# Two transformer blocks on one core: in seven FFNs, gate and up blocks as seven block products in place of eight, with weight sums made by adding transfers

## What is computed

```python
def swiglu(x, w_gate, w_up, w_down):
    return (jax.nn.silu(x @ w_gate) * (x @ w_up)) @ w_down

for l in range(DEPTH):
    x = x + 0.5 * swiglu(rmsnorm(x, ffn1_norm[l]), ffn1_w_gate[l], ffn1_w_up[l], ffn1_w_down[l])
    x = x + hybrid_mixer(rmsnorm(x, mix_norm[l]), ...)
    x = x + 0.5 * swiglu(rmsnorm(x, ffn2_norm[l]), ffn2_w_gate[l], ffn2_w_up[l], ffn2_w_down[l])
```

## Time and profile before

| | us |
|---|---|
| median of 3 runs | 2456.77 (2456.68 to 2456.95) |
| profiled execution, span | 2455.0 |
| PE busy | 2426.3 (99%) |
| DVE busy | 1559.7 (64%) |
| ACT busy | 1183.0 (48%) |
| POOL busy | 205.5 (8%) |
| SP's queue, 433.23 MB | 49.2% of 16 DMA engines |
| POOL's queue, 67.65 MB | 8.6% of 16 DMA engines |

### The profile page before, as it was taken

One profiled execution on the slowest core, in us unless ns is written; L12 is line 12 of the kernel. 1 busy time (PEld: TensorE's weight loads), 2 busy tenths in 40 slices (PEclk: granted clock), 3 DMA queues, 4 the chain that ended last, 5 costly groups with the idle time before them and its releaser, 6 DMA issues.

```text
span 2455.0 us, 30703 instructions
## 1 busy us (share of the span) xinstructions
PE 2426.3 (99%) x12690; PEld 2069.7 (84%) x12690; DVE 1559.7 (64%) x1629; ACT 1183.0 (48%) x1276; POOL 205.5 (8%) x358
## 2 busy tenths in 40 slices
PE   8999999999999999999999999999999999999998
PEld 6889998888889988888889878888888898788887
DVE  6555876655656776565558657656665677577664
ACT  5435544434437544444435664544344356644442
POOL 0100200100100101101100010011011000100010
PEclk9999999999999999999999999999999999999999
DMA  8755447657654447657664445476576454454762
GB/s 334 238 209 189 156 165 246 227 209 237 236 204 181 164 148 272 227 205 259 227 214 174 161 154 206 180 262 231 202 256 231 172 184 152 150 208 159 256 232 101
DMA packets 82547, 504.42 MB, mean 205 GB/s; under 512 B 11608, under 2 KB 12760, under 8 KB 30184
## 3 DMA queue, kind: packets, MB, share of 16 engines
q1 hardware_dynamic: 61488, 433.23, 49.2%
q0 software_dynamic: 19744, 67.65, 8.6%
q10 hardware_dynamic: 1176, 1.58, 0.4%
HBM read 476.72 MB, written 25.69 MB: 205 GB/s over the span
## 4 chain that ended last, share of the span: by engine, by line
PE 91%; DVE 5%; ACT 3%; issue 1%; DMA 1%; SPq 0%; POOL 0%; DVEq 0%; POOLq 0%; ACTq 0%
PE acc L615 24%; PE acc L616 24%; PE acc L617 24%; PE acc L583 4%; PE acc L584 4%; PE acc L585 4%; DVE w_lo L516 2%; PE aux L799 1%; ACT w_hi L508 1%; DMA raw<-in_w 1%; ACT tmp L1484 1%; PE stat L633 1%; PE bc L633 0%; PE aux L1170 0%; PE aux L981 0%
## 5 line engine op out<-in xcount | busy, mean ns | idle before, releaser
L516 DVE TENSOR_TENSOR w_lo<-raw,w_hi 128x2048 fp32r<-128x2048 f32 (+1 forms) x417 | 934.3, 2244 | 672.3 <-ACT w_hi L508 671.5
L508 ACT ACTIVATE w_hi<-raw 128x2048 fp32r<-128x2048 f32 (+1 forms) x417 | 782.8, 1880 | 624.2 <-PE acc L617 594.0
L615 PE MATMUL acc<-w_hi,x_hi 128*128 128x512 f32 (+1 forms) x1848 | 720.4, 390 | 3.1 <-DVE x_lo L1736 2.1
L617 PE MATMUL acc<-w_lo,x_hi 128*128 128x512 f32 (+1 forms) x1848 | 715.6, 387 | 0.0
L616 PE MATMUL acc<-w_hi,x_lo 128*128 128x512 f32 (+1 forms) x1848 | 715.5, 387 | 0.0
L615 PEld LDWEIGHTS acc<-w_hi,x_hi 128*128 128x128 f32 x1848 | 347.1, 188 | 77.8 <-issue 6.1
L617 PEld LDWEIGHTS acc<-w_lo,x_hi 128*128 128x128 f32 x1848 | 347.0, 188 | 71.3
L616 PEld LDWEIGHTS acc<-w_hi,x_lo 128*128 128x128 f32 x1848 | 347.2, 188 | 70.4 <-issue 1.0
L615 PE MATMUL acc<-w_hi,h_parts 128*128 128x512 f32 x704 | 274.5, 390 | 0.0
L617 PE MATMUL acc<-w_lo,h_parts 128*128 128x512 f32 x704 | 273.9, 389 | 0.0
L616 PE MATMUL acc<-w_hi,h_parts 128*128 128x512 f32 x704 | 273.9, 389 | 0.0
(11 more groups left out here) (396 smaller groups left out, 2229.3 us busy)
## 6 DMA issues: line engine op xcount, KB each, us to landing
raw<-in_w SPq DMA_DIRECT2D x399, 1024.0 KB, 4.8
squares<-tmp POOLq DMA_DIRECT2D x40, 512.0 KB, 2.9
tmp<-squares POOLq DMA_DIRECT2D x160, 128.0 KB, 4.5
raw<-in_w SPq DMA_DIRECT2D x18, 512.0 KB, 3.6
tmp<-in_norm_gb POOLq DMA_DIRECT2D x8, 1024.0 KB, 5.4
tmp<-in_norm_gb POOLq DMA_DIRECT2D x6, 512.0 KB, 3.7
tmp<-in_gate_rows POOLq DMA_DIRECT2D x12, 256.0 KB, 3.1
squares<-tmp POOLq DMA_DIRECT2D x8, 256.0 KB, 2.3
```

The source lines that it names most:

```text
L508: nc.scalar.activation(w_hi[:, slot, 0:kind], raw[:, slot, 0:kind], ACT.Copy).then_inc(hi_done, 1)
L516: nc.vector.tensor_tensor(w_lo[:, slot, 0:kind], raw[:, slot, 0:kind], w_hi[:, slot, 0:kind].bitcast(F32), ALU.subtract).then_inc(lo_done, 1)
L615: nc.tensor.matmul(out, vh, wh, start=first and k == 0, stop=False)
L617: last = nc.tensor.matmul(out, vh, wl, start=False, stop=last_k and k == nk - 1)
```

## The change

In every FFN but the first, blocks 1 and 2 form a group, and blocks 3 and 4 another. Write X as four blocks, X11 and X12 (tokens 0 to 127, rows 0 to 511 and 512 to 1023 of the weights) and X21 and X22 (the other tokens), and the weights of the first block of the group as B11, B21 (gate) and B12, B22 (up). The 2 x 2 product takes eight block products; the group takes seven, each 12 matmuls of 512 columns (`product`): X11 B11, X12 B21, X22 T4, and products of the weight sums T1 = B12 + B11, T2 = T1 + B22, T3 = B22 + B12 and of B22 with four sums of x, where T4 = T2 + B21. The group's second block is done as before, its four chunks laid between the products. A group has eleven chunks (T1, B11, B22, gate 0, T2, B21, T3, gate 1, T4, up 0, up 1) in place of eight; PE works 180 matmuls for it in place of 192.

The four sums of x are X21 - X22 (for T1), X21 - X22 - X11 (T2), X11 - X21 (T3) and X12 + X21 - X22 - X11 (B22).

The weight sums are made by transfers: POOL issues a DMA that adds a weight chunk to what lies in the `raw` buffer. T2 is added onto T1 and T4 onto T2, T3 onto B22, each once the old content has been split; SP skips those chunks. T1 is a load and then an add.

The sums of x: POOL adds `x_hi` and `x_lo` and forms the four sums (`x_sums`, eight operations of 128x512), ACT rounds each (`sum_high`), DVE writes the remainder (`sum_low`). PE accumulates the products in the banks of `aux` and `bc`, where ACT and DVE copy and subtract in between (`kept`). Some semaphores are merged to make room.

```diff
-FFN = [WIDE] * (UP_CHUNKS + 5) + [HALF] * 2 + [WIDE] * 5
-SUBS = ["ffn", "mix1", "ffn"] * 2 + ["ffn", "mix2", "cross", "ffn"] * 2
-KINDS = {"ffn": FFN, "mix1": MIX1, "mix2": MIX2, "cross": CROSS}
-TILES = {"ffn": 26, "mix1": 30, "mix2": 46, "cross": 10}
+FFN0 = [WIDE] * (UP_CHUNKS + 5) + [HALF] * 2 + [WIDE] * 5
+FFN = [WIDE] * (UP_CHUNKS + 6 + 5) + [HALF] * 2 + [WIDE] * 5
+SUBS = ["ffn0", "mix1", "ffn"] + ["ffn", "mix1", "ffn"] + ["ffn", "mix2", "cross", "ffn"] * 2
...
+B11, B21, B12, B22 = range(4)
+GROUP = (((LOAD, B12), (ADD, B11)), ((LOAD, B11),), ((LOAD, B22),), ((LOAD, 4 + B11),),
+         ((ADD, B22),), ((LOAD, B21),), ((ADD, B12),), ((LOAD, 4 + B21),),
+         ((ADD, B21),), ((LOAD, 4 + B12),), ((LOAD, 4 + B22),))
+G_T1, G_B11, G_B22, G_GATE0, G_T2, G_B21, G_T3, G_GATE1, G_T4, G_UP0, G_UP1 = range(11)
+GROUPS = ((1, 4), (3, 15))
...
+            if moves[c][-1][0] == ADD:
+                act.wait_ge(added[sums.index(c) % 2], 16 * (sums.index(c) // 2 + 1))
+            else:
+                act.wait_ge(loaded[slot], 16 * landings[c])
...
+                how, place = moves[c][0]
+                if how == ADD:
+                    continue
...
+                def product(c, bank, v_hi, v_lo, first):
+                    chunk_ready(c)
+                    for k in range(4):
+                        wh, wl = wblock(c % RING, k, 512)
+                        nc.tensor.matmul(bank, v_hi[:, k], wh, start=first and k == 0, stop=False, skip_group_check=True)
+                        nc.tensor.matmul(bank, v_lo[:, k], wh, start=False, stop=False, skip_group_check=True)
+                        last = nc.tensor.matmul(bank, v_hi[:, k], wl, start=False, stop=k == 3, skip_group_check=True)
+                    last.then_inc(chunk_done, 1)
+                def group(g, b, tile):
+                    a_, b_, e_ = aux[:, 0, :], aux[:, 1, :], bc[:, :]
+                    x11, x12, _, x22 = ((x_hi[:, k, at], x_lo[:, k, at]) for k, at in X_AT)
+                    s1, s3, s2, s4 = zip(SUM_HI, SUM_LO)
+                    pe.wait_ge(sum_parts, 4 * (f - 1) + 1)
+                    if b:
+                        pe.wait_ge(outs_ready, 3 * b - 2)
+                    product(g + G_T1, e_, *s1, True)
+                    if b:
+                        pe.wait_ge(kept_silu, 2 * b)
+                    product(g + G_B11, b_, *x11, True)
+                    pe.wait_ge(sum_parts, 4 * f)
+                    pe.wait_ge(kept_copied, 3 * b + 1)
+                    product(g + G_B22, e_, *s4, False)
+                    both(g + G_GATE0, tile, 0)
+                    pe.wait_ge(kept_copied, 3 * b + 2)
+                    product(g + G_T2, b_, *s2, False)
+                    if b:
+                        pe.wait_ge(outs_ready, 3 * b - 1)
+                    product(g + G_B21, a_, *x12, True)
+                    pe.wait_ge(kept_copied, 3 * b + 3)
+                    product(g + G_T3, b_, *s3, False)
+                    both(g + G_GATE1, tile, 1)
+                    pe.wait_ge(outs_ready, 3 * b + 3)
+                    product(g + G_T4, b_, *x22, False)
+                    both(g + G_UP0, tile + 2, 0)
+                    both(g + G_UP1, tile + 2, 1)
                 if s:
                     skewed_in(s, c0, t0)
-                for j in range(4 if s else 0, UP_CHUNKS):
-                    both(c0 + j, t0 + 2 * (j // 2), j % 2)
-                    if s == 6 and j == 8:
-                        bias_rows()
+                    for n, (i, g) in enumerate(GROUPS):
+                        group(c0 + g, 2 * (f - 1) + n, t0 + 4 + 4 * n)
+                        if s == 6 and n == 0:
+                            bias_rows()
+                    for j in range(2):
...
+                def sum_high(q):
+                    act.wait_ge(sum_ready, 4 * (f - 1) + q + 1)
+                    nc.scalar.activation(SUM_HI[q], XQ4[SUM_AT[q]], ACT.Copy).then_inc(sum_hi, 1)
+                def kept(g, b, i):
+                    ended_chunk(act, g + G_T1)
+                    act.wait_ge(sum_parts, 4 * f)
+                    if i > 1:
+                        act.wait_ge(hid_ready, 12 * f + 2 * (i - 2) + 2)
+                    nc.scalar.activation(Q5B, bc[:, :], ACT.Copy).then_inc(kept_copied, 1)
+                    ahead.to(g + 4)
+                    ended_chunk(act, g + G_B11)
+                    nc.scalar.activation(P1B, aux[:, 1, :], ACT.Copy).then_inc(kept_copied, 1)
+                    ahead.to(g + 5)
                     if i > 1:
                         hid_high(i - 2)
-                    silu(i, 0)
-                    silu(i, 1)
-                    for j in range(1, 4 if i < 5 else 2):
-                        if s == 6 and i == 2 and j == 1:
-                            bias_copy()
-                        ahead.to(c0 + 4 * i + j + 4)
+                    ahead.to(g + 7)
+                    ended_chunk(act, g + G_T2)
+                    nc.scalar.activation(UB, aux[:, 1, :], ACT.Copy).then_inc(kept_copied, 1)
+                    ahead.to(g + 9)
+                    act.wait_ge(outs_ready, 3 * b + 2)
+                    nc.scalar.activation(P1B, P1B, ACT.Silu).then_inc(kept_silu, 1)
+                    ahead.to(g + 10)
+                    hid_high(i - 1)
+                    silu(i + 1, 0)
+                    silu(i + 1, 1)
+                    ahead.to(g + 11)
+                    ended_chunk(act, g + G_T4)
+                    nc.scalar.activation(G1B, aux[:, 1, :], ACT.Silu).then_inc(kept_silu, 1)
+                    ahead.to(g + 14)
+                def ups():
+                    if s == 0:
+                        ahead.to(c0 + 4)
+                    silu(0, 0)
+                    if s:
+                        sum_high(0)
+                    ahead.to(c0 + 4)
+                    if s:
+                        for q in range(1, 4):
+                            sum_high(q)
+                    silu(0, 1)
+                    ahead.to(c0 + 7)
+                    if s:
+                        for n, (i, g) in enumerate(GROUPS):
+                            kept(c0 + g, 2 * (f - 1) + n, i)
+                            if s == 6 and n == 0:
+                                bias_copy()
+                        return
...
+                def sum_low(q):
+                    dve.wait_ge(sum_hi, 4 * (f - 1) + q + 1)
+                    V_.tensor_tensor(SUM_LO[q], XQ4[SUM_AT[q]], SUM_HI[q].bitcast(F32), ALU.subtract).then_inc(sum_parts, 1)
+                def kept_times(i, tt, gates_, ups_, ready):
+                    n = 12 * f + 2 * i + tt
+                    dve.wait_ge(squares_ready, n - 1)
+                    dve.wait_ge(*ready)
+                    V_.tensor_tensor(HID[:, tt], gates_, ups_, ALU.mult).then_inc(hid_ready, 1)
+                    dve.wait_ge(hid_ready, n + 1)
+                def kept(g, b, i):
+                    ahead.to(g + 4)
                     if i > 1:
                         hid_low(i - 2)
-                    if i < 5:
+                    ahead.to(g + 7)
+                    dve.wait_ge(kept_copied, 3 * b + 3)
+                    V_.tensor_tensor(UB, bc[:, :], UB, ALU.subtract).then_inc(outs_ready, 1)
+                    ahead.to(g + 8)
+                    ended_chunk(dve, g + G_B21)
+                    dve.wait_ge(kept_copied, 3 * b + 2)
+                    V_.tensor_tensor(P1B, P1B, aux[:, 0, :], ALU.add).then_inc(outs_ready, 1)
+                    ahead.to(g + 9)
+                    ended_chunk(dve, g + G_T3)
+                    dve.wait_ge(kept_copied, 3 * b + 1)
+                    V_.tensor_tensor(Q5B, Q5B, aux[:, 1, :], ALU.subtract).then_inc(outs_ready, 1)
+                    dve.wait_ge(outs_ready, 3 * b + 1)
+                    kept_times(i, 0, P1B, UB, (kept_silu, 2 * b + 1))
+                    ahead.to(g + 10)
+                    hid_low(i - 1)
+                    ahead.to(g + 11)
+                    dve.wait_ge(outs_ready, 3 * b + 3)
+                    kept_times(i, 1, G1B, Q5B, (kept_silu, 2 * b + 2))
+                    turn_squares(i)
+                    ahead.to(g + 13)
+                    times(i + 1, 0)
+                    times(i + 1, 1)
+                    turn_squares(i + 1)
+                    ahead.to(g + 14)
+                def ups():
+                    if s == 0:
+                        ahead.to(c0 + 6)
+                    times(0, 0)
+                    if s:
+                        sum_low(0)
+                        ahead.to(c0 + 4)
+                        for q in range(1, 4):
+                            sum_low(q)
+                    ahead.to(c0 + 6)
+                    times(0, 1)
+                    turn_squares(0)
+                    ahead.to(c0 + 7)
+                    if s:
+                        for n, (i, g) in enumerate(GROUPS):
+                            kept(c0 + g, 2 * (f - 1) + n, i)
...
+            def add(c):
+                how, place = moves[c][-1]
+                if len(moves[c]) > 1:
```

(47 more changed lines are left out.)

209 lines of the change are left out of this document (135 added, 74 removed).

## The result

The changed kernel takes **2715.84 us** (median of 4 runs, 2711.21 to 2723.45) against 2456.72: a ratio of 1.1058, 95% interval 1.1044 to 1.1071. I had forecast 2474 with a range up to 2511. Slower was right, the size was not: 259 us are lost, not 17.

The account below looks back on a forecast made before the run. TensorE was taken as the bound (busy 2426.3 of 2455.0 us). -38.1 + 7 x (5.4 + 1.2 + 1.1) + 1.6 = +17.4 gave a span of 2472.4, plus 1.8 for the runs' median: 2474 us, range 2438 to 2511.

Parts of the forecast that it names:

- The matmuls: TensorE over seven FFNs: 168 fewer matmuls at 0.2267 us each save 38.1 us, a span of 2416.9 with nothing else.
- The start of the first group: Each FFN: POOL's sums of x delay chunk 5's split, so PE waits 5.4 us after T1.
- The 1.2 us in front of chunk 7: First ordinary chunk of each FFN's first group: DVE has 6.6 us of work against PE's 5.44, costing 1.2 us.
- 1.6 once: FFN of sublayer 6: three more transfers issued ahead of its sums of x cost 1.6 us once.
- The adding transfers: An add lands after 7.7 us; T4's costs 1.1 us per FFN in the first group, nothing in the second.
- T1 and T3 of the second group: No cost: T2 and T3 have 9 us and more, T1's add comes some 10 us before ACT wants it.
- Rival A: Adds move bytes twice and land after 9.6 us, delaying T4: 2497 us, 2511 at 10.6; chance with beyond 0.20.
- The sign that I gave for being wrong: Wrong on the adds if ACT never waits for DMA at T2 or T4, or several microseconds in every group.
- B: Start of the first group: the sums of x hide, both waits go, the whole 38.1 is won: 2419 us; chance 0.10.
- C: POOL is not held by DVE and adds are as cheap as loads: 2447 us; chance 0.14.
- D: Gain and waits cancel within 5 us, with T4 in time: 2457 us; chance 0.14.

Follow-up runs that it names:

- run 6: The changed kernel with its 56 adding transfers left out (weight sums missing), sums of x still on POOL: 2468.28 us.
- run 7: run 6 with the sums of x on VectorE and the splits of chunks 5 and 6 moved ahead: 2417.71 us.
- run 2: The changed kernel with its adding transfers overwriting instead of adding, in the same places (weight sums missing): 2597.55 us.
- Run 4: The changed kernel with the squares' store on SP's queue, ahead of the load of a later chunk: 2637.49 us.
- run 5: The changed kernel with T4's add ahead of the permutation, sums of x on VectorE and the squares' store on SP's queue: 2589.52 us.
- run 8: run 5 with the 56 transfers overwriting instead of adding (weight sums missing): 2494.35 us.
- 10: The changed kernel with T1 by load and adding transfer (14 adds), the other weight sums and the sums of x on VectorE: 2510.9 us.
- 12: 10 with T1 by adding transfer in the first group only (7 adds), by VectorE in the second: 2466.45 us.
- run 1: The changed kernel with T4's add issued ahead of the permutation in both groups: 2629.71 us.
- 13: 12 with VectorE splitting the second group's B11 earlier: 2472.41 us.
- 14: 12 with the transposes of the squares behind the next ordinary chunk's split, at the start of both groups: 2466.84 us.
- 15: 14 with POOL forming the low halves of three blocks' hidden values: 2471.45 us.
- run 11: 10 with two of the eight operations of the sums of x on POOL: 2518.07 us.

## Why the prediction was wrong, step by step

- **The matmuls: right.** -38.1 forecast; without adds and with VectorE's sums the span is 2416.0, forecast 2416.9 for "nothing else". (The pages count 12690 and 12522 matmuls, 168 fewer, as the listing does.)
- **The start of the first group: the wait right, the total partly by luck.** POOL's operations take 1.29 us alone and up to 3.33 beside a low split, as worked out from the earlier trace rows, and PE waits for chunk 5's low split: 5.4 us forecast, 4.8 measured. The 1.2 us in front of chunk 7 never show. Behind the wait PE ran at the low clock, so B11's matmuls took from 394.97 to 399.21, 4.2 us in place of 2.72, and chunk 7's low split (the first of two in 4.45 us from 399.10) was in time. Forecast 47.8 us (7 x 6.6 and 1.6 once), measured 50.6 by runs 6 and 7: 18.0 us of it are longer busy time, which I had priced at nothing, and it fills the place of what the waits lack.
- **The adding transfers: the failed step.** 7 x 1.1 = 7.7 us forecast, 247.5 measured. PE's wait in front of T4 was to be 1.1 us in the first group and nothing in the second; it is 11.4 to 16.1 us in both. Four things in it were wrong. *(a) Its landing:* 7.7 us taken, at most 10.6. T4's adds take 13.2 to 15.5. The price of adding doesn't explain that: plain, in the same place, they take 13.8 (run 2), while the other plain ones mostly land after 5 to 6. I priced a transfer by itself and not among the four loads ahead of it on its queue and SP's loads beside it. *(b) What stands ahead of it:* I gave the squares' store 2.9 to 4.9 us. It lands after 9.7 to 14.7, since T3's add lies in front of it on its queue and in the DMA engines, and T4's add is issued only then. Run 4 alone gives 78 us back. I counted that add's cost to ACT and not to what stands behind it. *(c) The bytes:* I compared 360 GB/s (463 with adds counted twice) with 420 and let the run-ahead of eight chunks carry the rest. Runs 5, 8 and 7 show 95 us for adding and 77 us for the bytes, with the order of run 5. *(d) The clock:* I counted a wait at its length. Behind the waits TensorE's clock was down: its busy time is 61.5 us longer than its matmuls need, 43.6 of it with the adds (2449.7 against 2406.1 in run 6).
- **T1 and T3 of the second group: not priced.** I gave T2 and T3 "9 us and more"; the add of the second group's T3 lands after 11.2 to 11.5 us, and PE waits 14.7 us for it over seven FFNs. I wrote that T1's add comes "some 10 us before ACT wants it", which holds for the first group alone; runs 10 and 12 put 44 us on the second's.
- **Rival A** had the direction and half of the mechanism (an add takes the engines nearly twice as long), but the wrong size (2497 to 2511): it kept the issue times of a queue in which nothing is late. The sign that I gave for being wrong, ACT waiting for DMA several microseconds in every group, is what the waits show (328.6 us, 53 times).
- **B, C and D** are out. B wanted POOL's sums to hide; run 6 has them without adds and loses 50.6 us. B's bound of 2419, no wait at all, is reached with VectorE's sums (run 7, 2417.7). C wanted POOL unheld and adds as quick as loads, and neither is so. D wanted gain and waits to cancel within 5 us: even without adds run 6 is 11.4 us above the kernel before.

What stays open: which of its neighbours make T4's transfer so late. Ahead of the squares' loads a plain one takes 8.1 to 10.9 us (run 8, where the store is on SP's queue as well), an adding one still 12.1 to 16.0 (run 1). How the 77 us of plain transfers divide between bandwidth and the order in which they go out was not taken apart. That VectorE's amount of work bounds 12 is argued from its busy time and from 13 to 15; no run had less of it without using POOL.

## What to carry to other kernels

A transfer inside a chain (a store that its reader waits for, a second transfer into a buffer) must be priced at its landing with everything that the change puts in front of it on its queue, and the steps behind it shifted by that; a median of the quiet profile is a lower bound, and a median over all transfers of the new kernel can hide the few that are waited for (9.4 over 56, 14.4 for T4's). Before adding by DMA, ask whether the operands already lie in SBUF: here T3 written as T2 - B11 spared every second load, and took back 232 of 259 us. Look at the helper engine in the stage and not on average: VectorE is busy 64% of the time before, but with the splits of a group it has 35.5 us of work in 40.8, and with the weight sums 42.4 to 44.7. With the latter no exact version kept the 38 us that TensorE saves.

## What the runs showed of the hardware

- An adding transfer of HBM into SBUF holds the DMA engines 5.3 us a megabyte, an overwriting one on the same queue 2.9 (the change and run 2). Its issue holds POOL 0.90 us (median of 56), a plain one 0.56.
- The store of 512 KB on POOL's queue lands after 9.7 us with the adds (median of 40), after 5.4 from SP's queue beside the same adds, 5.0 with plain transfers in their place, 3.0 without them.
- A transfer of 1 MB issued right behind the four loads of the squares, beside SP's loads, lands after 14.4 us adding and 13.8 plain (medians of 14).
- After the wait of 4.50 us that ended at 394.97 TensorE ran at 1.2 GHz (0.43 us a matmul) to 397.70 and then at 2.4 (0.23); over the kernel 238 us more of waits came with 61.5 us more busy time.
- VectorE and POOL with two SBUF inputs each took turns in both directions: POOL's operation 3.33 us in place of 1.30 beside a low split, and VectorE's two 3.95 in place of 1.29 beside POOL's two (run 11). The Trainium skill, "SBUF — State Buffer", section "Who interferes with whom", calls their shared port pair an exclusive lock; these rows agree.
